# Recurrence of a hybrid encoder layer: the order of the 64x64 products on the two halves of the TensorE array

## The reference, cut to what matters

```python
def rwkv7_step(S, inp):
    r, w, k, v, a, b = inp
    sa = jnp.einsum('dbhvk,dbhk->dbhv', S, a)
    S = S * w[..., None, :] + sa[..., None] * b[..., None, :] + v[..., :, None] * k[..., None, :]
    y = jnp.einsum('dbhvk,dbhk->dbhv', S, r)
    return S, y
...
    S0 = jnp.zeros((N_DIRS, B, H, N, N), jnp.float32)
    _, y = lax.scan(rwkv7_step, S0, xs)
```

## Time and profile before

| | |
|---|---|
| median of three runs | 3472.36 us |
| profiled execution, its own time | 3467.95 us |
| its span, from first to last instruction | 3466.1 us |
| mean granted TensorE clock | 0.946 of full |
| PE busy | 3073.6 us, 89% of the span |
| PEld busy | 2465.4 us, 71% |
| DVE, ACT, POOL busy | 1556.1, 1070.8, 795.3 us |

### The profile page before, as it was taken

One profiled execution on the slowest core, in us unless ns is written; L12 is line 12 of the kernel. 1 busy time (PEld: TensorE's weight loads), 2 busy tenths in 40 slices (PEclk: granted clock), 3 DMA queues, 4 the chain that ended last, 5 costly groups with the idle time before them and its releaser, 6 DMA issues. The chain is left out here.

```text
span 3466.1 us, 64119 instructions
## 1 busy us (share of the span) xinstructions
PE 3073.6 (89%) x26764; PEld 2465.4 (71%) x26764; DVE 1556.1 (45%) x1959; ACT 1070.8 (31%) x2041; POOL 795.3 (23%) x937
## 2 busy tenths in 40 slices
PE   5777998999654999999698599999999999799999
PEld 2555556888334998999366478888888888688887
DVE  2555552333674555543454364444444444333333
ACT  2333552111542444443234231111111111222222
POOL 2342551000448665671232330000000000000000
PEclk7988999999876999999899799999999999899999
DMA  4222112332473333311754321111111111631331
GB/s 111 91 85 67 37 37 60 73 73 49 169 288 122 107 110 104 110 53 33 241 162 151 119 85 49 48 48 48 48 48 47 47 46 41 233 97 48 96 96 36
DMA packets 210014, 313.19 MB, mean 90 GB/s; under 512 B 63193, under 2 KB 134233, under 8 KB 206714
## 3 DMA queue, kind: packets, MB, share of 16 engines
q1 hardware_dynamic: 208346, 308.74, 27.9%
q10 hardware_dynamic: 1440, 1.18, 0.1%
HBM read 208.16 MB, written 101.71 MB: 89 GB/s over the span
## 5 line engine op out<-in xcount | busy, mean ns | idle before, releaser
L91 PE MATMUL up_p<-h_hi,up_w_hi 128*128 128x512 f32 x1408 | 550.4, 391 | 41.7 <-DVE h_lo L1962 38.8
L92 PE MATMUL up_p<-h_lo,up_w_hi 128*128 128x512 f32 x1408 | 549.7, 390 | 0.0
L93 PE MATMUL up_p<-h_hi,up_w_lo 128*128 128x512 f32 x1408 | 549.4, 390 | 0.0
L91 PEld LDWEIGHTS up_p<-h_hi,up_w_hi 128*128 128x128 f32 x1408 | 265.5, 189 | 99.5 <-issue 44.5
L1914 ACT COPY up_raw<-up_p 128x512 f32<-128x512 f32 x176 | 103.3, 588 | 749.0 <-PE up_p L93 749.0
L93 PEld LDWEIGHTS up_p<-h_hi,up_w_lo 128*128 128x128 f32 x1408 | 265.5, 189 | 55.6
L92 PEld LDWEIGHTS up_p<-h_lo,up_w_hi 128*128 128x128 f32 x1408 | 265.6, 189 | 55.2
L91 PE MATMUL down_p<-down_act_hi,down_w_hi 128*128 128x512 f32 x704 | 274.8, 390 | 23.1 <-DVE down_act_lo L2119 23.1
L1972 DVE TENSOR_SCALAR up_con<-up_raw,vecs_sb 128x2048 f32<-128x2048 f32 x44 | 59.3, 1347 | 514.6 <-ACT up_raw L1914 514.6
L92 PE MATMUL down_p<-down_act_lo,down_w_hi 128*128 128x512 f32 x704 | 274.5, 390 | 0.0
L93 PE MATMUL down_p<-down_act_hi,down_w_lo 128*128 128x512 f32 x704 | 274.3, 390 | 0.0
(11 more groups left out here) (232 smaller groups left out, 6334.9 us busy)
## 6 DMA issues: line engine op xcount, KB each, us to landing
rec_inp<-gate_chunks SPq DMA_DIRECT2D x64, 512.0 KB, 3.6
up_w<-in_w_up SPq DMA_DIRECT2D x44, 512.0 KB, 4.2
act_out<-up_con SPq DMA_DIRECT2D x22, 1024.0 KB, 4.3
down_act<-act_out SPq DMA_DIRECT2D x88, 256.0 KB, 3.2
gate_chunks<-gates_out SPq DMA_DIRECT2D x4, 4096.0 KB, 12.8
first_w<-in_w_attn SPq DMA_DIRECT2D x24, 512.0 KB, 3.6
rkv_chunks<-rwkv_project_mix SPq DMA_DIRECT2D x12, 1024.0 KB, 6.4
gate_chunks<-gates_out SPq DMA_DIRECT2D x4, 3072.0 KB, 11.7
```

The lines of the kernel that those rows point to most:

```text
L91: pe.matmul(out, w_hi, x_hi, start=start, stop=False)
L92: pe.matmul(out, w_hi, x_lo, start=False, stop=False)
L93: return pe.matmul(out, w_lo, x_hi, start=False, stop=stop)
```

## The change

The order of the products within a call. Before, each unit's upper product was followed by the same unit's lower product. Now a call issues all products of the upper half for units 0 to 3 first, and then all of the lower half for units 0 to 3. In the calls with several products to be added (x, h, y), a unit's products of one half stand together. Operands, results, number of instructions, waits, the increment on the last product and the order of the calls are as they were. ak, rb, u, gram, cross and corner go through `each`, tok and v through `turned`.

```diff
-                def pair(to, lhs, rhs, start=True, stop=True):
-
+                def one(to, lhs, rhs, rows, u, start, stop):
+
+                    return pe.matmul(to[rows, u], lhs[rows, u], rhs[rows, u], start=start, stop=stop)
+
+                def each(to, lhs, rhs):
                     for rows in HALVES:
-                        mm = pe.matmul(to[rows], lhs[rows], rhs[rows], start=start, stop=stop)
+                        for u in range(RU):
+                            mm = pe.matmul(to[rows, u], lhs[rows, u], rhs[rows, u], start=True, stop=True)
                     return mm
 
-                def each(to, lhs, rhs):
-                    for u in range(RU):
-                        mm = pair(to[:, u], lhs[:, u], rhs[:, u])
-                    return mm
-
                 def turned(to, x):
-                    for u in range(RU):
-                        for rows in HALVES:
+                    for rows in HALVES:
+                        for u in range(RU):
                             mm = pe.matmul(to[rows, u], x[rows, u], ident[rows, rows], start=True, stop=True)
                     return mm
...
                     to = bank[d][0][:, :, 0:L]
-                    for u in range(RU):
-                        if c > 0:
-                            pair(to[:, u], ar[d][:, c % RING, u, 0:L], H[d][:, c % 2, u], True, False)
-                        mm = pair(to[:, u], akrk[d][:, c % 2, u, 0:L], vtok[d][:, u], c == 0, True)
+                    for rows in HALVES:
+                        for u in range(RU):
+                            if c > 0:
+                                one(to, ar[d][:, c % RING, :, 0:L], H[d][:, c % 2], rows, u, True, False)
+                            mm = one(to, akrk[d][:, c % 2, :, 0:L], vtok[d], rows, u, c == 0, True)
                     mm.then_inc(S["x"][d], 1)
...
                     to = bank[d][1][:, :, 0:L]
-                    for u in range(RU):
-                        pair(to[:, u], vtok[d][:, u], akrk[d][:, c % 2, u, L:], True, False)
-                        if c > 0:
-                            pair(to[:, u], H[d][:, c % 2, u], ar[d][:, c % RING, u, L:], False, False)
-                        mm = pair(to[:, u], us[d][:, u], rb[d][:, c % 2, u], False, True)
+                    for rows in HALVES:
+                        for u in range(RU):
+                            one(to, vtok[d], akrk[d][:, c % 2, :, L:], rows, u, True, False)
+                            if c > 0:
+                                one(to, H[d][:, c % 2], ar[d][:, c % RING, :, L:], rows, u, False, False)
+                            mm = one(to, us[d], rb[d][:, c % 2], rows, u, False, True)
                     mm.then_inc(S["y"][d], 1)
```

More of the change, by code:

```diff
@@ L1150, in h_part @@
                     to = bank[d][0][:, :, 0:L]
-                    for u in range(RU):
-                        pair(to[:, u], toks[d][:, u, 1], vtok[d][:, u], True, False)
-                        mm = pair(to[:, u], toks[d][:, u, 0], us[d][:, u], False, True)
+                    for rows in HALVES:
+                        for u in range(RU):
+                            one(to, toks[d][:, :, 1], vtok[d], rows, u, True, False)
+                            mm = one(to, toks[d][:, :, 0], us[d], rows, u, False, True)
                     mm.then_inc(S["h"][d], 1)
```

## The result

The changed kernel takes 3608.96 us (median of 4 runs, 3605.79 to 3613.13) against 3470.18 us for the kernel before beside it: ratio 1.0403, 95% interval 1.0389 to 1.0418, +138.8 us. The forecast was slower, +292 us.

A forecast was written before the change was run, and what follows sets the result against it. TensorE was taken to bound the recurrence's 544 us. Two records overlapping at each change of half gave +302, less 10 for the copy of y: +292 us, 3764 us from the median of the runs, range 3575 to 3885.

The forecast's parts named there:

- What bounds the kernel: Recurrence's main stretch, 544.0 us: TensorE is the bound, PE busy 512.3 us, and whatever it does more slowly is paid in full.
- The mechanism: Main stretch: halves served one after the other, one to four records overlapping at each change of half; chance 0.83.
- independent streams: Rival for the recurrence: TensorE serves both halves independently whatever the order, no change, 3472 us; chance 0.10.
- strict order: Recurrence: records start in program order, so one record overlaps at each change of half; +395 us.
- a step of 107 ns at every record: Rival for the recurrence: loads exposed, each record pays its load, 107 instead of 58 ns; +1101 us, 4573 us; chance 0.03.
- 14880 records by 58.2 ns: Main stretch: 14880 records outside ak, each 58.2 ns on its half, less the overlapped ones in each run.
- v = 1: Main stretch with one record overlapping at each change of half: 882 us, +395; one end of the range.
- v = 2: Main stretch with two records overlapping at each change of half, the value taken: 789 us, +302.
- v = 3: Main stretch with three records overlapping at each change of half: 696 us, +209.
- The issue waits (20.5 us) I leave as they are: PE's waits for nothing that the profile shows (14.8 and 5.7 us) were taken to stay unchanged.
- The wait for y's copy gone: PE's 10.0 us wait for ACT's copy of y should go, the v call between becoming longer than the copy.
- Early calls at nothing: The 24 calls ahead of the main stretch, under POOL, may add 6 us at most; none was taken.

The follow-up runs named there:

- Experiment 7: Kernel before, with the lower half's products left out of y only (24 records in place of 48): 3450.35 us against 3466.37, ratio 0.9957.
- 1: Changed kernel with each unit's upper products ahead of its lower ones in all calls, runs no longer than six: 3466.71 us against 3467.79, ratio 0.9999.
- 6: Kernel before with the gram call moved ahead of cross in the order of calls: 3455.17 us against 3463.25, ratio 0.9973.
- 3: Changed kernel with only y keeping the new order (runs of 24), all other calls in runs of 2 or 4: 3510.57 us, ratio 1.0121.
- 2: Changed kernel with halves changing after every two units, runs of 4, 8 in x and h, 12 in y: 3500.92 us, ratio 1.0105.
- 4: Changed kernel with only one-product calls keeping the new order (runs of 8), x, h and y in runs of 4, 4, 6: 3498.49 us, ratio 1.0097.
- experiment 5: Kernel before, with every product of the lower half left out of the whole recurrence: 3823.05 us against 3463.25, ratio 1.1033.
- 8: Changed kernel, each call beginning with the half the last one ended with, one change of half per call: 4418.03 us, ratio to before 1.2749.

## Why the prediction was right in kind and wrong in size

- **What bounds the kernel:** right. TensorE was the bound of the 544 us, and what it does more slowly is paid there and nowhere else. Experiment 7 shows that the halves work at the same time, as argued from 54.6 against 111 ns.
- **The mechanism:** right. At a change of half a fixed number of records overlaps, and a run pays for what is left. Neither independent streams (calls would have stayed at 0.467) nor strict order occurred, nor a step of 107 ns at every record (calls of 1.5 us and more). That step, which the prediction read after idleness, does occur once for each run of 64-column records in the changed kernel, at its first record, and the sum had no term for it; it is what makes three of four. 14880 records by 58.2 ns was the right base. The Trainium skill ("TensorE: Matmul & The Clock Gate", Part 3, The mechanism) has matmuls start strictly in order, which would be the 882 us of v = 1, and a window 64 deep, which holds for loads alone; only if it is read for the products too would it give the 487 us that the prediction drew from it. The trace has 685.9 us and agrees with neither time.
- **The step that failed: "I take v = 2".** It is three in net, four that overlap less the long first step. By the prediction's own sum v = 3 is +209 in place of +302 us, 93 of the 153 us missed. The step read rows after idleness, where the third record of a half may not have arrived yet the earlier trace rows, and one change of call with runs of two, where no more than two could pass. A lower bound was taken for the value. The bounds asked for both sides, v = 1 to 4, held it.
- **The second, smaller one: "The issue waits (20.5 us) I leave as they are".** They are zero after, and so is PE's idle time in the main part as a whole. The sum should have been made against PE's rate (487 us), not against the stretch (544): 487 + 209 = 696 us for the main part, 10 us from the 685.9 measured, where the prediction had some 840. The table accounts for these 10 us and more: 62 ak calls 0.105 us under the rule (6.5 us), 124 cross and corner calls 0.062 under it (7.7 us); the clock, at half until about 1108, adds some 3.3 us.
- Together: 302 - 10 = 292 was forecast, where the 10 is the wait for y's copy. 209 - 57 - 10 = 142 was found in the main part, where the 57 (544 - 487) holds that wait and this 10 is what the calls take under the rule.
- **The wait for y's copy gone:** right. **Early calls at nothing:** right. PE's busy time ahead of 1101.1 grew from 22.85 to 31.60 us, 1.5 of them by the main part's earlier start, and that start came no later for it. **The 12.6 us for rec_side** were counted among the waits of the main part, but lie ahead of it; no term of the sum used them.
- **Signs named beforehand:** tok calls 0.70 apart were forecast, 0.575 found; PE busy at about 95%, found 100%; clock 0.98, found 0.99.

Where the 57 us lay before is seen in part: 31.7 us are PE's idle time, and some 9 are lost to the clock. Here is one such place, two windows of the kernel before, right behind an issue wait of 1.84 us that ends at 1331.97:

```profile
1332.00:1334.00 2.00, 2.00 (x49) 2.00 (x50) 0.00 (x0) 0.37 (x1) 1.84 (x4) 0.67 0.18 61
1334.00:1336.00 2.00, 2.00 (x44) 2.00 (x42) 0.00 (x0) 0.74 (x2) 2.00 (x4) 0.50 0.08 22
```

Of the 2 us windows between 1102 and 1646, 12 have a clock under 0.97, and their shortfall adds up to 9.4 us; after, only the first four do, 3.3 us. Of the other 16 us some 10 lie beside the named waits: PE counts as busy until its last record's modelled end, so the 51 gaps of over 0.23 us between two starts add up to 42.8 us and not to 31.7. That leaves some 6 us, of which gaps of 0.12 to 0.23 us (23 of them, 3.3 us) can hold a part.

**Open.** What lets a new run begin when three records of the old one haven't started, and not earlier, wasn't separated: a queue of three for each half and a window over the program's order give the same times here. Nor was it shown what makes a run's first step long. That the issue waits are a supply of instructions which a slower TensorE no longer outruns fits all runs (20.5 us before, 22.3 in 1, 17.5 in 6, 12.2 in 3, 10.8 in 7, 3.4 in 2, 2.0 in 4, none after), but no run changed that supply itself.

## What to carry to other kernels

Where a kernel works on two row halves of the array, order its instructions so that a run on one half is no longer than six records of 64 columns (three float32 products). In this kernel the order was free up to there. From runs of 8 on, each further record of a run cost 58 ns in place of 29, less whatever TensorE was idle for anyway; runs of 7 weren't tried. Make such a sum against the engine's rate, not against the time of a stretch: idle time that isn't tied to a named wait goes first. Look at the granted clock in every run, since leaving work out (experiment 5) or making runs longer still (8) left it at half here.

## What the runs showed that wasn't expected

- **The clock can stay at the lower level with PE busy all the time.** In experiments 5 and 8 it was granted 0.50 in the whole recurrence, with PE busy 100%; in the kernel after, with PE equally busy, 1.00 from 1110 on. All three have 0.50 to 0.54 ahead of the main part; in the kernel after it rises within 9 us, in 5 and 8 not before the recurrence ends. What the two have in common is that the halves rarely work together: never in 5, and once per call in 8 against twice after. Whether that is the cause was not shown. Its price is the largest here: 4418.03 against 3608.96 us.
- **Half the products, the same time.** y with 24 records takes the 1.400 us of y with 48 (experiment 7).
- **Overtaking over three records, between halves.** The first upper record of a call starts at 1085.38, ahead of three lower ones that stand before it in the program (1085.43, .49 and .55), so 0.17 us ahead of the last of them.
- **Waits that vanish when the engine that waits gets slower:** 20.5 us of issue waits before, none after, with the same 15,900 or so records.
